# Mixer of a hybrid trunk: rows of x from a second, host-turned layout in place of turns on TensorE

## The reference, cut to what matters

```python
def rms_norm(x, g):
    y = x * lax.rsqrt(jnp.mean(x * x, axis=-1, keepdims=True) + RMS_EPS)
    return y * g
h = rms_norm(x, mix_norm_g)          # (1024, 1024)
proj = h @ w_in                      # (1024, 2312): q, k, v, z, xBC, dt
# ... q, k normed; windowed attention with sinks; conv, SSD scan, gate, norm
x = x + jnp.concatenate([y_attn, y_ssm], axis=-1) @ w_out
```

## Time and profile before

| what | us |
|---|---|
| median of 3 runs | 2100.13 |
| the runs | 2082.68, 2100.13, 2100.52 |
| the profiled execution, its own time | 2083.14 |
| its span | 2081.3 |
| outside the span | 1.8 |

### The profile page before, as it was taken

How to read it: one execution, slowest core, us unless ns; L and a number is a source line. 1 busy time by engine, 2 the same in 40 slices (tenths; PEclk the granted TensorE clock), 3 DMA queues, 4 the chain that set the end, 5 groups by cost and what they waited for, 6 DMA issues and landing times. The chain is left out here.

```text
span 2081.3 us, 47130 instructions
## 1 busy us (share of the span) xinstructions
PE 1879.5 (90%) x20636; PEld 1153.3 (55%) x20636; DVE 882.7 (42%) x1980; ACT 429.2 (21%) x965; POOL 427.1 (21%) x546
## 2 busy tenths in 40 slices
PE   7899999998699998898969999799969999898992
PEld 5666667664566655555635444345546665555651
DVE  2665565565721111111116899893271111111114
ACT  3332322234311110110114122143411111010110
POOL 2111100111222332222213011120222232221220
PEclk9999999999799999999989999899979999999996
DMA  9100000030699999999968455512289999999996
GB/s 312 37 1 1 1 0 0 0 122 17 254 377 423 422 424 426 425 425 425 421 250 254 100 110 127 121 31 81 81 326 401 416 424 424 428 422 424 423 390 257
DMA packets 89992, 520.60 MB, mean 250 GB/s; under 512 B 23062, under 2 KB 46666, under 8 KB 72384
## 3 DMA queue, kind: packets, MB, share of 16 engines
q1 hardware_dynamic: 63976, 457.76, 53.7%
q0 software_dynamic: 24064, 51.45, 9.0%
q10 hardware_dynamic: 1752, 8.44, 1.0%
HBM read 491.31 MB, written 34.65 MB: 253 GB/s over the span
## 5 line engine op out<-in xcount | busy, mean ns | idle before, releaser
L1367 PE MATMUL ps<-wgu,xT 128*32 128x256 f32 x7168 | 419.0, 387 | 35.1 <-issue 35.1
L1532 DVE TENSOR_TENSOR hh<-sg,ps 128x128 f32<-128x128 f32 x168 | 66.5, 396 | 704.5 <-ACT sg L1189 704.1
L1367 PEld LDWEIGHTS ps<-wgu,xT 128*32 128x32 f32 x7168 | 238.7, 112 | 192.2 <-issue 56.6
L1252 POOL DMA_INDIRECT y_rows<-my,yidx x168 | 166.6, 992 | 736.5 <-ACT my L1183 729.2
L1367 PE MATMUL ps<-early_gu,xT 128*32 128x256 f32 x3584 | 213.3, 392 | 14.9 <-issue 12.3
L1382 PE MATMUL ps<-wd,hhT 128*32 128x256 f32 x3584 | 213.8, 379 | 0.0
L1189 ACT ACTIVATE sg<-ps 128x128 f32<-128x128 f32 x168 | 46.6, 277 | 687.1 <-PE ps L1367 687.1
L1367 PEld LDWEIGHTS ps<-early_gu,xT 128*32 128x32 f32 x3584 | 118.9, 113 | 97.5 <-issue 27.7
L1382 PEld LDWEIGHTS ps<-wd,hhT 128*32 128x32 f32 x3584 | 119.6, 110 | 73.8
L2098 DVE SCALAR_TENSOR_TENSOR conv<-dd,par,conv 128x256 f32<-128x256 f32 (+1 forms) x255 | 131.5, 593 | 0.2
L787 PE MATMUL ps<-hn,early_gu 128*128 128x128 f32 x1024 | 116.8, 275 | 0.0
(11 more groups left out here) (344 smaller groups left out, 2110.9 us busy)
## 6 DMA issues: line engine op xcount, KB each, us to landing
wgu<-in_moe_w_gate_up SPq DMA_DIRECT2D x42, 4096.0 KB, 31.6
early_gu<-in_moe_w_gate_up SPq DMA_DIRECT2D x22, 4096.0 KB, 30.8
wd<-in_moe_w_down SPq DMA_DIRECT2D x42, 2048.0 KB, 29.9
early_wd<-in_moe_w_down SPq DMA_DIRECT2D x22, 2048.0 KB, 29.0
early_wd<-in_conv_w_pw SPq DMA_DIRECT2D x22, 512.0 KB, 5.5
conv<-prod POOLq DMA_DIRECT2D x20, 512.0 KB, 4.5
h_rows<-wgu ACTq DMA_DIRECT2D x8, 1024.0 KB, 3.9
early_gu<-in_w_in SPq DMA_DIRECT2D x2, 2048.0 KB, 16.7
```

The costliest lines, as they stand in the source:

```text
L1252: pool.indirect_dma_start(out=y_quarters, out_offset=bass.IndirectOffsetOnAxis(ap=yidx[:, tl, q:q + 1], axis=0), in_=y[:, n % YB, :], in_o ...
L1367: mm = pe.matmul(ps[TB * g:TB * g + TB, GU + n % 2, 0:2 * P].rearrange("p (a f) -> p a f", a=2), xT[:, q % 2, j, TB * tl:TB * tl + TB], wg ...
L1532: tt(hh[:, n % 2, :].rearrange("q (k f) -> q k f", k=KF), by_k(sg[:, n % 2, :]), by_k(ps[:, GU + n % 2, P:2 * P]), ALU.mult).then_inc(hh_r ...
```

## The change

The host hands over two more inputs. `x_turned` holds each tile of x with channels on partitions (512 KB a tile); `mixer_rows` holds the nine small rows already turned, so that one DMA fills `par`. A tile of h now comes as xT (DMA) times norm weight (in place), times a row of roots along the free dimension, into `hT`. `hn`, its transposes and the evacuation are gone. The row of roots is needed on every partition: for tiles 0 and 1 PE turns a broadcast column of `rstd` into PSUM (`turn_rstd`); for tiles 2 to 7 SP stores the roots to a DRAM scratch, waits, and loads them back broadcast to all partitions. The weight product runs on DVE for tiles 0 and 1 and on POOL, once in each of turns 0 to 5, for the rest. There is one `xT` buffer. The k/v projection of tile 1 moves to the place that it has in other turns.

```diff
         def _(sp):
             sp.dma_start(x[:, 0, :], tiles[:, 0, :]).then_inc(x0_loaded, 16)
-            sp.dma_start(w_in[:, :, Q0:K0], w[:, :, 0:512]).then_inc(wq_loaded, 16)
+            sp.dma_start(xT[:], I["x_turned"][0]).then_inc(xT_loaded, 16)
+            for half in range(2):
+                sp.dma_start(w_q[:, half, :, :], w[:, 4 * half:4 * half + 4, 0:512]).then_inc(wq_loaded[half], 16)
             sp.dma_start(w_in[:, :, K0:DT0], w[:, :, 512:768]).then_inc(wkv_loaded, 16)
             sp.dma_start(w_in[:, :, DT0:Z0], w[:, :, 2304:2312]).then_inc(wkv_loaded, 16)
+            sp.dma_start(w_z, w[:, :, 768:1280]).then_inc(wz_loaded, 16)
             sp.dma_start(x[:, 1, :], tiles[:, 1, :]).then_inc(x1_loaded, 16)
-            sp.dma_start(w_z, w[:, :, 768:1280]).then_inc(wz_loaded, 16)
+            sp.wait_ge(hT_ready, 2)
+            sp.dma_start(xT[:], I["x_turned"][1]).then_inc(xT_loaded, 16)
...
+            sp.wait_ge(hT_ready, 4)
+            sp.dma_start(xT[:], I["x_turned"][2]).then_inc(xT_loaded, 16)
+            sp.wait_ge(rstd_ready, 3)
+                sp.dma_start(k.rstd_rows.rearrange("n p -> p n")[:, 2:NT], rstd[:, 2:NT]).then_inc(rstd_stored, 16)
+            sp.wait_ge(rstd_stored, 16)
+            sp.dma_start(rstd_rows[:, 2:NT, :]..., k.rstd_rows[2:NT, :]...partition_broadcast(P)).then_inc(rstd_spread, 16)
             load_router(k, sp, 0)
+            for c in range(3, NT):
+                sp.wait_ge(hT_ready, 2 * c)
+                sp.dma_start(xT[:], I["x_turned"][c]).then_inc(xT_loaded, 16)
...
         # POOL, in a turn, behind xde and ahead of qk_rstd_and_dt
+                if nxt2:
+                    pool.wait_ge(xT_loaded, 16 * (c + 3))
+                    take_wait()
+                    pool.tensor_tensor(xT[:], xT[:], par[:, :, G_IN:G_IN + 1].to_broadcast([P, KD, P]), ALU.mult).then_inc(xT_scaled, 1)
...
         # ACT: nine DMAs into rows become one
+            act.dma_start(par[:], I["mixer_rows"]).then_inc(par_loaded, 16)
...
         # DVE
+            def normalise(c, row):
+                for half in range(2):
+                    dve.tensor_tensor(hT[:, 4 * half:4 * half + 4, :], xT[:, 4 * half:4 * half + 4, :], row.to_broadcast([P, 4, P]), ALU.mult).then_inc(hT_ready, 1)
...
             halo(0, 0)
-            dve.wait_ge(rstd_ready, 3)
             dve.wait_ge(small_loaded, 16 * 4)
+            dve.wait_ge(rstd_spread, 16)
...
                 if nxt2:
                     dve.wait_ge(x1_projected, c + 2)
-                    normalise(c + 2, p)
+                    dve.wait_ge(xT_scaled, c + 1)
+                    normalise(c + 2, rstd_rows[:, at(c + 2), :])
...
         # PE
+            def turn_rstd(c):
+                pe.wait_ge(rstd_ready, c + 1)
+                pe.transpose(ps[:, B6 + c, 0:P], rstd[:, c:c + 1].to_broadcast([P, P]), ident[:]).then_inc(rstd_turned, 1)
...
-                if first:
-                    turn_hn(c + 1, 1 - p)
...
-                if first:
-                    pe.wait_ge(x0_out, 1)
-                    project(c + 1, 1 - p, PJ1, K0, Z0, kv_projected)
...
-                if nxt and not first:
+                if nxt:
                     project(c + 1, 1 - p, PJ1, K0, Z0, kv_projected)
...
-                project_part(c, p, 0, 0, KD)
-                if nxt is not None:
-                    turn_hn(*nxt)
-                project_part(c, p, 1, 0, KD)
+                for half in range(2):
+                    project_part(c, p, half, 0, KD)
```

More of the change, by code:

```diff
@@ L595, in _, with scale_first, normalise_first @@
         def _(dve):
[L596 to L600, removed]
+            def scale_first(c):
+                dve.wait_ge(xT_loaded, 16 * c + 16)
+                link(dve.tensor_tensor(xT[:], xT[:], par[:, :, G_IN:G_IN + 1].to_broadcast([P, KD, P]), ALU.mult))
+            def normalise(c, row):
                 for half in range(2):
-                    dve.tensor_tensor(hT[:, 4 * half:4 * half + 4, :], ps[:, TR + half, :].rearrange("p (k t) -> p k t", k=4),
-                                      par[:, 4 * half:4 * half + 4, G_IN:G_IN + 1].to_broadcast([P, 4, P]), ALU.mult).then_inc(hT_ready, 1)
+                    dve.tensor_tensor(hT[:, 4 * half:4 * half + 4, :], xT[:, 4 * half:4 * half + 4, :], row.to_broadcast([P, 4, P]), ALU.mult).then_inc(hT_ready, 1)
+            def normalise_first(c):
+                dve.wait_ge(rstd_turned, c + 1)
+                normalise(c, ps[:, B6 + c, 0:P].unsqueeze(1))
             def qk_norm(c):
@@ L637, in _ @@
             link = Link(dve, dve_link)
[L638 to L645, removed]
+            dve.wait_ge(par_loaded, 16)
+            scale_first(0)
+            normalise_first(0)
+            dve.wait_ge(hT_ready, 2)
             qk_norm(0)
+            scale_first(1)
             convolve(0, 0, 0)
             dve.wait_ge(x1_projected, 1)
-            dve.wait_ge(rstd_ready, 2)
-            normalise(1, 1)
-            hT_evacuate(1, 1)
+            normalise_first(1)
             convolve(0, 0, 1)
             halo(0, 0)
-            dve.wait_ge(rstd_ready, 3)
             dve.wait_ge(small_loaded, 16 * 4)
-            BEFORE, TURN = 0, 15
+            dve.wait_ge(rstd_spread, 16)
+            BEFORE, TURN = link.n, 15
             def scores(c, p, g):
@@ L791, in _ @@
             pe.wait_ge(ident_ready, 1)
[L792 to L800, removed]
+            def turn_rstd(c):
+                pe.wait_ge(rstd_ready, c + 1)
+                pe.transpose(ps[:, B6 + c, 0:P], rstd[:, c:c + 1].to_broadcast([P, P]), ident[:]).then_inc(rstd_turned, 1)
+            turn_rstd(0)
+            for half in range(2):
+                pe.wait_ge(hT_ready, half + 1)
+                pe.wait_ge(wq_loaded[half], 16)
+                for j in range(4 * half, 4 * half + 4):
+                    mm = pe.matmul(ps[:, PJ0, :], hT[:, j, :], w_in[:, j, Q0:K0], start=(j == 0), stop=(j == KD - 1))
+            mm.then_inc(q_projected, 1)
             pe.wait_ge(wkv_loaded, 32)
@@ L805, in _ @@
             project(0, 0, PJ0, Z0, X0, z_projected)
+            turn_rstd(1)
             pe.wait_ge(wx_loaded[0], 16)
@@ L839, in project_part, with project_out @@
                     mm.then_inc(o_done, 1)
-            def project_out(c, p, nxt=None):
+            def project_out(c, p):
                 pe.wait_ge(wo_loaded, 16 * 3)
@@ L939, in turn @@
                     pe.wait_ge(x0_out, c + 2)
-                if not first:
-                    if nxt:
-                        pe.wait_ge(y_out, c + 1)
-                        project_out(c - 1, 1 - p, (c + 2, p) if nxt2 else None)
-                elif nxt2:
-                    turn_hn(c + 2, p)
+                if nxt and not first:
+                    pe.wait_ge(y_out, c + 1)
+                    project_out(c - 1, 1 - p)
             turns(pe, turn)
@@ L2145, with turned_layouts @@
           "moe_w_down"]
+def turned_layouts(inputs):
+    x_turned = np.asarray(inputs["x"]).reshape(NT, P, KD, P).transpose(0, 3, 2, 1)
+    rows = np.zeros((ROWS, D), np.float32)
+    rows[G_IN] = np.asarray(inputs["mix_norm_g"]).reshape(D)
+    rows[CONV_B] = np.asarray(inputs["ssm_conv_b"]).reshape(D)
+    rows[CONV_W:CONV_W + SCONV] = np.asarray(inputs["ssm_conv_w"]).reshape(SCONV, D)
+    rows[G_SSM] = np.tile(np.asarray(inputs["ssm_out_norm_g"]).reshape(DI), 2)
+    rows[G_QK, 0:P] = np.tile(np.asarray(inputs["q_norm_g"]).reshape(DH), 2)
+    rows[G_QK, P:2 * P] = np.tile(np.asarray(inputs["k_norm_g"]).reshape(DH), 2)
+    return {"x_turned": x_turned, "mixer_rows": rows.reshape(ROWS, KD, P).transpose(2, 1, 0)}
 def kernel(**inputs):
@@ L2153 @@
     arrays, aps = {}, {}
-    for name in INPUTS:
-        a = np.ascontiguousarray(inputs[name])
+    for name, a in list({n: inputs[n] for n in INPUTS}.items()) + list(turned_layouts(inputs).items()):
+        a = np.ascontiguousarray(a)
         arrays[f"in_{name}"] = a
```

35 lines of the change are left out of this document (13 added, 22 removed).

## The result

The changed kernel takes 2115.84 us (median of 4 runs, 2112.21 to 2119.37), the kernel before, in the same series, 2097.65 (4 runs, 2082.68 to 2100.52). The ratio is 1.0114, with a 95% interval of 1.0066 to 1.0161. It is slower, by just over the 1% that I had set as the edge of "no change" (I gave that 0.11), and 7 us above my figure of 2108.8, inside the range. From median to median the change costs 18.2 us, where I had 8.7. The two profiled executions lie further apart: 2114.82 against 2083.14, spans 2113.1 and 2081.3. Most of what follows is about why these 31.8 us are two different things, and only the first of them is the change.

The account below looks back on a forecast made before the run. TensorE, busy 90% of the span, was taken as the bound, with its waits and the start. Terms 10.65 - 7.1 + 5.2 = +8.7 us on the median 2100.13 gave 2108.8, range 2088 to 2122.

Parts of the forecast that it names:

- First matmul: Start: first projection at about 9 instead of 12.76 us, counted as no gain; at most 3.8.
- Step A: Start: 1.05 MB more queued ahead of x, then the roots' DRAM round trip; DVE's turn 0 at 67.5 instead of 55.0.
- Step B: Turn 0 to first turns of probabilities: L825 at 87.9 against 77.25 us, 10.65 later.
- Step C: Turn 0 to turn 1: the product writes hT itself, 8.5 instead of 15.7 us; wins 7.1.
- Step D: Steady turns: transposes gone win 0.87 us, POOL's product delays L679 by 1.9; five times, +5.2.
- Rival 1: Steady turns: DVE not held by POOL's product, L679 may start first; -2.7 us, 2097.4; chance 0.15.
- The other case that I had allowed for: Steady turns: L679 up to 2.3 us later, not 1.7, if a small operation ahead is held as well.
- Sum for the mixer: Whole mixer: 10.65 - 7.1 + 5.2 = +8.7 us.
- Rival 2: Start: roots' round trip far longer, DVE's turn 0 at about 80, 12.3 us later; +21 us, 2121; chance 0.10.
- rival 3: Start not lengthened, extra 1.05 MB fits into gaps; about -0.5 us, 2099.6; chance 0.13.
- After the mixer every step hangs on mixer events and moves with it.: Everything behind the mixer: shifts with the mixer's +8.7 us.

Follow-up runs that it names:

- wout_behind: Changed kernel with the three DMAs of w_out (4 MB) issued behind the roots' store and load instead of ahead; mixer's end 531.12 us, against 530.36 in the changed kernel.
- kv_early: Changed kernel with the k/v projection of tile 1 ahead of cb again, as before the change; mixer's end 528.84 us.
- after_again: Changed kernel, unchanged, run again beside the kernel before: 2114.76, 2097.59, 2111.75, 2110.88 us; mixer's end 527.46.
- the two filler runs: Unused TensorE matmuls added in the first router stage: changed kernel with three reorderings and w_out's DMAs later, 2074.77 us; kernel before, 2091.60 us.

## Why the prediction was right or wrong

**First matmul.** Right: 9.11. It gained nothing, as said; TensorE then waited 7.1 us for ACT's copy behind the squares.

**Step A.** The landing (47.5 forecast, 47.9 measured), the roots (56.8, 57.04) and the load (3.9, 3.9) came out. The term that was mis-sized is the store: I took 6.7 us from ready roots to its landing, built from the queue's end plus 1.9, and bounded it by g_moe's 5.4 behind that queue. Measured were 10.3, and 9.7 with 4 MB less in the queue. A load of 1024 single elements was no measure for a store of 768 into DRAM, and the queue that I added to it was no part of the price, as wout_behind shows. DVE's turn 0 began at 71.20 instead of 67.5, inside the bound of 73.4, but by luck: 5.4 behind the queue comes to 10.2 from ready roots, near the measured 10.3 for a wrong reason. 3.7 us of the miss of 5.6 in the mixer are from here. The page of the Trainium skill that I weighed (DMA: Bandwidth & Descriptors, Rules for kernel authors) pointed the right way with one descriptor for each element. Its fixed cost of about 2.0 us stands in the section on the anatomy of one DMA, which is about DMAs that GpSimd issues, while these are SP's, and the estimate by it, 66.6, was further off than mine from rows.

**Step B.** L825 was forecast at 87.9 and L839 came at 92.25, of which 3.7 is the start. From scores to L839 it took 19.85 against 15.5 + 1.8 + 1.9 = 19.2. That the new place of the k/v projection costs nothing was assumed there, and kv_early bears it out.

**Step C.** Won 5.5 instead of 7.1 (15.0 late at L839, 9.54 late at the end of tile 2's q projection: the turns of y behind it start at 124.05 against 114.51). The product and the projection took what I said; the difference is TensorE's clock after the wait of 2.37: 8.11 for the first 64 matmuls of x/B/C instead of 7.31, 1.94 for the turns instead of 1.04. In after_again the same way was 1.6 us shorter (90.40 to 120.57) with the same wait, so this part differs from run to run.

**Step D.** The mechanism was right: POOL's next operation with no gap behind `xde`, DVE's product held until it ended, TensorE paying it in full, in six turns. The price was a little less: 1.45 for each turn, for POOL's product took 1.91 and not 2.08. A steady turn became 0.57 us longer (60.82 against 60.25) where I had 1.03. One turn of the five took 62.41, at a lower mean clock, and with it the five together cost 4.4 against my 5.2. Rival 1 did not happen in any turn: L679 never came first, since POOL started 0.3 us ahead of it. The other case that I had allowed for, a small DVE operation ahead of L679 held as well, is in after_again: in turn 2 an operation on 4 columns (L695) took 1.87, and TensorE waited 2.8.

**Sum for the mixer.** +14.3 against +8.7; with the second profile of each kernel it is +11.4 to +14.7, so the miss is 2.7 to 6.0, and the 1.6 of step C and the 0.7 of step B are smaller than the scatter. Rival 2 (roots far slower) was the right direction for the miss, at under a third of the size it would have needed (3.7 of 12.3); rival 3 was wrong, the landing did move.

**"After the mixer every step hangs on mixer events and moves with it."** Right for the work, and wrong for the time: the router stage ran at the other clock. I had seen that the profiled execution lay 17 us below the median of the same program and had put my figure on the median, without knowing what the 17 us were. That is why 2108.8 is only 7 off, while the same +8.7 on the profiled execution (2091.8) is 23 off its counterpart. The offset was argued then; the two filler runs show what it is. That the figure for the median came so near is in part luck: the 2100.13 that I started from lay in before's upper group, and all four runs of the changed kernel came out in its upper group too, which I had no reason to expect.

Whether the change itself makes the lower clock more frequent stays open: 1 of 8 runs in the lower group against 23 of 49 is a hint, and no run was made for it.

## What to carry to other kernels

Where an engine already waits for a DVE product of two SBUF operands, do not put a GpSimd operation right ahead of it: place it where DVE is idle, and the same work costs next to nothing (10.9 to 12.7 us won here by a move of four lines). Put a wait at the first use, not at the head of the stage. Compare stages between marks, not two totals, and take a second profile to see how far a mark scatters (up to 2.9 us here): the total held a stage whose clock fell in some runs of a kernel and not in others.

## What the runs showed that I had not expected

- A stage in which TensorE is busy 100% of the time can sit at the lower clock level to its end (26.00 of 26.00 us busy at 0.50), when the work is turns of 128 and matmuls of 36 columns. With three matmuls of 512 columns at its start and one for each tile, 20 of 20 runs show no upper group, and both profiles have 1.00 there. Which of the two fillers does it was not tried.
- A store of 768 single 4-byte elements to DRAM took 9.4 to 10.4 us until the next DMA that waits for it, in ten profiles, while a load of 1024 such elements landed in 5.4 and, in the changed kernel, in 4.0.
- DMAs issued behind a transfer on the same queue slowed it: without w_out's 4 MB behind them, the 3 MB of x of the changed kernel landed at 45.2 instead of 47.4 to 48.4 (seven profiles).
